# Shifting x by the mean of two feature tiles ahead of the block's product, and summing the block norm's squares on TensorE

## The reference

```python
def layer_norm(x, g, b):
    mu = jnp.mean(x, axis=-1, keepdims=True)
    var = jnp.mean(jnp.square(x - mu), axis=-1, keepdims=True)
    return (x - mu) * lax.rsqrt(var + LN_EPS) * g + b

def swiglu_ffn(x, w_gu, w_down):
    a, u = jnp.split(x @ w_gu, 2, axis=-1)
    return (jax.nn.silu(a) * u) @ w_down

for l in range(2):
    x = layer_norm(ALPHA * x + 0.5 * swiglu_ffn(x, ...), ln1_g[l], ln1_b[l])
    x = layer_norm(ALPHA * x + hybrid_mixer(x, ...), ln2_g[l], ln2_b[l])
    x = layer_norm(ALPHA * x + 0.5 * swiglu_ffn(x, ...), ln3_g[l], ln3_b[l])
```

```python
h = concatenate([meta, x])                      # 528 tokens
h = h + 0.5 * swiglu(rmsnorm(h, ffn1_norm), ...)
h = h + (differential attention | sparse attention over the 128 best keys) @ w_out
h = h + 0.5 * swiglu(rmsnorm(h, ffn2_norm), ...)
return h[:, 16:]
```

## Time and profile before

| | us |
|---|---|
| Median of three runs | 3179.1 |
| The profiled execution | 3178.52 |
| Its span, first to last instruction | 3177.1 |
| TensorE (PE) busy in it | 3067.3 |
| VectorE (DVE) busy | 1416.9 |
| ScalarE (ACT) busy | 1179.3 |
| GpSimd (POOL) busy | 372.4 |
| Mean granted clock of TensorE, as a share of full speed | 0.987 |

### The profile page before, as it was taken

How to read it: one execution, slowest core, us unless ns; L and a number is a source line. 1 busy time by engine, 2 the same in 40 slices (tenths; PEclk the granted TensorE clock), 3 DMA queues, 4 the chain that set the end, 5 groups by cost and what they waited for, 6 DMA issues and landing times.

```text
span 3177.1 us, 39372 instructions
## 1 busy us (share of the span) xinstructions
PE 3067.3 (97%) x16470; PEld 2564.3 (81%) x16470; DVE 1416.9 (45%) x2118; ACT 1179.3 (37%) x1914; POOL 372.4 (12%) x275
## 2 busy tenths in 40 slices
PE   9999999999999999999999999999999789799999
PEld 7888876888888888886788888899998657688888
DVE  3332455643335333375573333644323666554432
ACT  3322366433214222265552222522223456442321
POOL 0000133300001000033310001100014122110000
PEclk9999999999999999999999999999999899899999
DMA  4223221232232323331222233222233101122232
GB/s 157 93 92 92 97 87 54 67 107 93 91 97 78 107 93 89 97 108 54 67 81 99 93 91 95 69 91 91 84 93 108 34 27 41 34 87 93 98 88 80
DMA packets 76496, 269.62 MB, mean 85 GB/s; under 512 B 8720, under 2 KB 9008, under 8 KB 76064
## 3 DMA queue, kind: packets, MB, share of 16 engines
q1 hardware_dynamic: 74448, 260.08, 25.4%
q0 software_dynamic: 1872, 7.04, 0.7%
HBM read 264.97 MB, written 2.11 MB: 84 GB/s over the span
## 4 chain that ended last, share of the span: by engine, by line
PE 88%; DVE 6%; ACT 4%; issue 1%; DMA 0%; POOL 0%; SPq 0%; DVEq 0%; ACTq 0%
PE psum L339 25%; PE psum L342 24%; PE psum L345 24%; PE psum L400 3%; PE psum L412 2%; PE psum L362 1%; PE psum L358 1%; PE psum L360 1%; PE psum L636 1%; ACT w_hi L284 1%; DVE x_lo L703 1%; PE psum L2599 1%; DVE b_rank L2874 1%; ACT prob L1729 0%; DVE x L788 0%
## 5 line engine op out<-in xcount | busy, mean ns | idle before, releaser
L295 DVE TENSOR_TENSOR w_lo<-w_raw,w_hi 128x1024 fp32r<-128x1024 f32 (+1 forms) x442 | 551.5, 1250 | 1246.7 <-ACT w_hi L284 1246.6
L339 PE MATMUL psum<-x_hi,w_hi 128*128 128x512 f32 (+1 forms) x2792 | 967.9, 371 | 8.6 <-ACT neg_mean L2670 5.2
L342 PE MATMUL psum<-x_hi,w_lo 128*128 128x512 f32 (+1 forms) x2792 | 951.1, 365 | 0.0
L345 PE MATMUL psum<-x_lo,w_hi 128*128 128x512 f32 (+1 forms) x2792 | 946.3, 363 | 0.0
L284 ACT CAST w_hi<-w_raw 128x1024 fp32r<-128x1024 f32 (+1 forms) x490 | 504.0, 1029 | 1170.9 <-PE psum L345 1134.3
L339 PEld LDWEIGHTS psum<-x_hi,w_hi 128*128 128x128 f32 x2792 | 503.2, 190 | 114.2 <-issue 16.8
L342 PEld LDWEIGHTS psum<-x_hi,w_lo 128*128 128x128 f32 x2792 | 502.4, 190 | 87.7 <-issue 5.7
L345 PEld LDWEIGHTS psum<-x_lo,w_hi 128*128 128x128 f32 x2792 | 503.0, 190 | 84.4
L339 PE MATMUL psum<-h_hi_ffn,w_hi 128*128 128x512 f32 (+1 forms) x792 | 296.9, 375 | 0.0
L342 PE MATMUL psum<-h_hi_ffn,w_lo 128*128 128x512 f32 (+1 forms) x792 | 292.2, 369 | 0.0
L345 PE MATMUL psum<-h_lo_ffn,w_hi 128*128 128x512 f32 (+1 forms) x792 | 290.7, 367 | 0.0
(11 more groups left out here) (384 smaller groups left out, 3440.9 us busy)
## 6 DMA issues: line engine op xcount, KB each, us to landing
w_raw<-in_ffn_gu SPq DMA_DIRECT2D x176, 512.0 KB, 3.2
w_raw<-in_ffn_down SPq DMA_DIRECT2D x64, 512.0 KB, 3.5
w_raw<-in_w_in SPq DMA_DIRECT2D x44, 512.0 KB, 3.3
w_raw<-in_b_gate SPq DMA_DIRECT2D x44, 512.0 KB, 3.2
w_raw<-in_b_up SPq DMA_DIRECT2D x44, 512.0 KB, 3.3
w_raw<-in_b_down SPq DMA_DIRECT2D x32, 512.0 KB, 3.5
w_raw<-in_ffn_down SPq DMA_DIRECT2D x32, 384.0 KB, 3.1
w_raw<-in_b_in SPq DMA_DIRECT2D x24, 512.0 KB, 3.3
```

The costliest lines, as they stand in the source:

```text
L295: nc.vector.tensor_tensor(w_lo[s][:, 0:n], w_raw[r][:, 0:n], w_hi[s][:, 0:n].bitcast(F32), ALU.subtract).then_inc(*w_low_dve.inc(u))
L339: nc.tensor.matmul(out, w_h, hi[:, c], start=first and i == 0, stop=False)
L342: nc.tensor.matmul(out, w_l, hi[:, c], start=False, stop=False)
L345: done = nc.tensor.matmul(out, w_h, lo[:, c], start=False, stop=final and i == n - 1)
```

## The change

Four things, told by where they stand.

1. `FfnNorm` (four stages) and `MixerNorm` (two) take the early mean from x tiles 0 and 1 of the stage's input. GpSimd adds the two (one 512-wide add), TensorE multiplies the sum with the ones (one 512-wide float32 matmul) before up-piece 20, or at 18.6 in mixer_1's timetable; ScalarE negates and scales it; VectorE does `x = scale x - mean` on eight tiles as single instructions at every second step from s = 24 on, or from 19.2 to 21.3 in mixer_1. The additions of the product to x become plain ones. The shifts and the mean matmul of before go. In a feed-forward stage ScalarE now squares one tile per down tile, and GpSimd adds x tile and square in turn; the sum of x for tiles 0 to 6 comes whole from `z_sum`, where tile 6 had its own two 256-wide matmuls before.
2. At the end of mixer_1 two weight roundings on ScalarE stand one and two tiles earlier, and the sums of part 1 (`pe_sums(1)`) stand after the third instead of the second `x_hi`/`x_lo` step of the next stage.
3. `BlockNorm`: TensorE sums each squared tile as soon as it is there (16 float32 matmuls of 256 columns, accumulated), and the 14 GpSimd additions and the two 264-wide sums go. `x_hi` comes from the scaled x with a bias of its own (`shift2`), before x gets its bias. The mean is copied to SBUF and the centring reads it there. The meta tokens' part of the second norm (their `x_hi`, `x_lo`, squares, sum in eight 16-column matmuls, root) is done in the middle of ffn2_1.
4. The timetables of the mixers are written as starts and lags. In mixer_2 the sums come out in another order of rounding, by which some steps with the same number change places.

```diff
+    if leave.first_mean and i == 20:
+        leave.pe_first_mean()
...
+    if leave.before_block and s == 12:
+        leave.act_meta()
+    if leave.first_mean and s == 22:
+        leave.act_first_mean()
...
+    if leave.before_block and s == 15:
+        leave.dve_meta()
+    if leave.first_mean and 24 <= s < 24 + 2 * KT and s % 2 == 0:
+        leave.dve_shift((s - 24) // 2)
...
+            def pool_pair(self):
+                nc.gpsimd.tensor_tensor(neg_mean[:, TOK], x[:, 0, TOK], x[:, 1, TOK],
+                                        ALU.add).then_inc(*self.paired.inc(0))
+            def pe_mean(self, out):
+                pe.wait_ge(*self.paired.at(0))
+                nc.tensor.matmul(out, ones[:], neg_mean[:, TOK], start=True,
+                                 stop=True).then_inc(*self.mean_summed.inc(0))
+            def act_negate(self, product):
+                nc.scalar.mul(neg_mean[:, TOK], product,
+                              -self.scale / (2 * P)).then_inc(*self.negated.inc(0))
+            def dve_shift(self, m):
+                nc.vector.scalar_tensor_tensor(
+                    x[:, m, TOK], x[:, m, TOK], self.scale, neg_mean[:, TOK],
+                    ALU.mult, ALU.add).then_inc(*self.shifted.inc(m))
...
         class SecondNorm(LateRoot):
+            def pe_square(self, k, part):
+                if k == 0:
+                    pe.wait_ge(*self.first.mean_copied.at(part))
+                pe.wait_ge(*self.first.sq2.at((k, part)))
+                done = self.first.pe_sum(256, self.squares[k % 3], part, k == 0, k == KT - 1)
+                done.then_inc(*self.first.sq2_summed.inc((k, part)))
+            def pe_within(self, part, step):
+                k = step if step < 2 else step - 2
+                if part < 2 and step not in (2, 3):
+                    if k:
+                        self.pe_square(k - 1, part)
+                    elif part:
+                        self.pe_square(KT - 1, 0)
+                if (part, step) == (2, 0):
+                    self.pe_square(KT - 1, 1)
...
             def act_out(self, k, part):
                 act.wait_ge(*self.scaled.at((k, part)))
+                nc.scalar.activation(x_hi[:, k, c], x[:, k, c], ACT.Identity,
+                                     bias=shift2[:, k:k + 1], scale=gain(second.g, k))
                 nc.scalar.activation(x[:, k, c], x[:, k, c], ACT.Identity,
                                      bias=gain(self.b, k)).then_inc(*self.moved.inc((k, part)))
+                if k >= 3:
+                    act.wait_ge(*self.sq2_summed.at((k - 3, part)))
-                nc.scalar.mul(x_hi[:, k, full], x[:, k, full], gain(self.second.g, k))
-                if k >= 3:
-                    act.wait_ge(*self.total2.at((k - 2, part)))
...
         class MixerNorm
             def pe_within(self, part, k):
-                if (part, k) == (0, 1):
+                if (part, k) == (0, 2):
                     self.pe_sums(1)
             def end_dve(self):
-                for m in range(2):
-                    self.dve_shift(m)
                 for m in range(KT):
-                    if m + 2 < KT:
-                        self.dve_shift(m + 2)
+                    self.dve_second(m, 0)
                     if m == 1:
                         dve_split(self.u_second + OUT_PAIRS - 1)
-                    self.dve_second(m, 0)
...
         mixer_2
-                order += [(s, "b_score", i), ..., (s + 0.65, "b_turn", i), (s + 0.7, "b_inverse", i),
-                          (s + 0.75, "b_copy", i), (s + 0.95, "b_value", i), ...]
+ 'b': [('b_score', 0), ..., ('b_turn', 0.65), ('b_inverse', 0.7), ('b_copy', 0.75), ('b_value', 0.95), ...]
```

More of the change, by code:

```diff
@@ L1428, in timetable @@
[L1428 to L1441 removed]
+                    follow(ended(tile), "value", v)
@@ L2215, in timetable, with follow @@
                 order = []
+                def follow(at, what, item):
+                    order.extend((at + lag, step, item) for step, lag in LAGS_2[what])
                 for tile in range(IN_TILES_2):
```

429 lines of the change are left out of this document (220 added, 209 removed).

## The result

The changed kernel takes 3185.17 us in the median of 11 runs (3183.54 to 3188.99); the kernel before, on the same chip, 3179.1 (11 runs, 3172.67 to 3182.46). The ratio is 1.0020, with a 95% interval of 1.0011 to 1.0029: slower by 6 us, 3.5 to 9. I had forecast 3179 and no change. The measured time lies in the range of 3168 to 3188, but outside the forecast's own 3175 to 3184, and the change is not none.

The account below looks back on a forecast made before the run. TensorE was taken to bound the kernel. Terms 0 (feed-forward), +0.4 (seams), -0.6 (block norm), +1.6 (meta tokens) and -0.5 (mixer_2) gave +0.9 on 3178.52 us: 3179 us, no change, range 3168 to 3188, the forecast's own 3175 to 3184.

Parts of the forecast that it names:

- That TensorE bounds, and each part must be read where TensorE waits: Whole kernel: TensorE is busy 3067.3 of 3177.1 us, so an edit pays only where it waits or its work changes.
- Seams of mixer_1, +0.4: Two seams of mixer_1: the wait for L1252 stays, later part-1 sums add 0.2 us each; bounds -1.5 and +3.
- one rival only: Seams of mixer_1 do shorten: each gives back its 4.84 us wait and 1.0 us of clock, to 3168; chance 0.14.
- Meta tokens, +1.6: ffn2_1: eight matmuls of 16 columns that no pause of TensorE takes in cost 1.6 us.
- mixer_2, -0.5: mixer_2: seven neighbouring pairs change places on TensorE, -0.5 us in all; bounds -4 and +6.
- The block norm, -0.6: Block norm: 16 new sums lie mostly in TensorE's pauses and other steps come earlier, -0.6 us; bounds -2.3 and +6.
- the case that I had given 0.07: Block norm: filled pauses hold TensorE's full clock, -1.7 us more, to 3177.5; chance 0.07.
- the pace there is set by ScalarE and VectorE, one tile in 1.28 us: Block norm: a TensorE step with its sum takes 1.13 us at full clock, less than the 1.28 us pace.
- The prediction's own sign, a steady step over 1.3 us: Block norm: a steady step over 1.3 us was named as a sign that the forecast is wrong.
- The half microsecond that I took off: Block norm: `x_hi` before the bias has one ScalarE operation of 0.5 us less; TensorE enters L412 about 0.5 us sooner.
- The feed-forward stages, 0: Four feed-forward stages: TensorE's work is equal and single shifts find room on VectorE, 0 each; bounds together -1 and +3.
- The bound of 0.3%: Whole kernel: run to run, less than about 0.3%, 9.5 us, can't be told from no change; chance of within 0.73.

Follow-up runs that it names:

- the four kernels: One group: none of block norm with meta tokens, seam order, table 3180.1 us; seam order and table 3181.2; block norm and table 3182.6; block norm and seam order 3185.6.
- the ten with the long wait: Profiled executions of ten kernels, before and changed included, with the long wait at mixer_1's seam; granted clock behind it 0.56 in the changed kernel, 0.70 to 0.79 in nine others.

## Why the prediction was wrong

The forecast was no change, from terms of 0, +0.4, -0.6, +1.6 and -0.5. The steps that failed are three of them: the block norm, whose pace was read from the kernel before; the seams, where the later sums were taken as half covered; and the feed-forward stages, taken as equal work. The two others held.

- **That TensorE bounds, and each part must be read where TensorE waits:** right. The 6.9 us of its new busy time hold the meta matmuls (1.7), the sums, the slower reads and what the clock took and gave; its waits stayed the same in sum.
- **Seams of mixer_1, +0.4: the wait was right, its price was not.** That the wait hangs on the list behind the reciprocal is shown twice: 4.86 and 4.84 us of wait without the shifts, 2.33 with another order. (The count of that list left out the additions L1258 that stand behind each L1252; they don't change the argument.) The later sums, at 0.2 us a seam, were the wrong part: the times put 2.1 us (uncertainty 1.1) on the new order of both seams, and half covered was assumed without a row. The clock behind the wait was left out of the sum. I had it in one rival only, as 1.0 us to be won, from a window that ends at 630; from 627 to 634 it is (1 - 0.76) x 7 = 1.7. In the profiled pair, from the restart to 700 and 1700, the two seams cost 2.7 us together.
- **Meta tokens, +1.6:** right. In the view of TensorE after, 16 records for eight matmuls until the next product,

```profile
1739.31 1.85 PE L1231 MATMUL psum<-square,ones 128*128 128x16 f32 x16
1741.01 0.48 PE L392 MATMUL psum<-x_hi,w_hi 128*128 128x512 f32 x1
```

  1741.01 - 1739.31 = 1.70 us.
- **mixer_2, -0.5:** +5.2 on both sides of it, so 0.0 in that execution; the times of the four kernels give -1.0 (uncertainty 1.1), with which the term agrees.
- **The block norm, -0.6: this step failed.** The sums are mostly hidden, as I said. The clock stayed full: from 1985 to 2035 the granted clock was 0.93 in all six executions with the old block norm, 1.00 in six with the new one and 0.97 in the seventh, so the case that I had given 0.07 is the one that came. The rule of the Trainium skill that the prediction quotes ("TensorE: Matmul & The Clock Gate", Part 1) agrees with that. It should have been a gain. But "the pace there is set by ScalarE and VectorE, one tile in 1.28 us" was taken over for the changed kernel, in which ScalarE's instructions are other ones. The prediction's own sign, a steady step over 1.3 us, came: 1.34 to 1.41. 16 tiles at 0.1 to 0.15 us more are an estimate of 1.6 to 2.4 us; the stretch became 0.9 longer in each of the six traces with the new block norm and single sums, with the lower clock of before (worth up to 1.7 us in the second of its two stretches) no longer in it. The half microsecond that I took off because `x_hi` comes before the bias doesn't exist for `x_lo`, for which TensorE waits. By the times, this term and the meta tokens together were 3.5 us (uncertainty 1.1), where I had 1.0. TensorE's rows, from the last steps to the third piece:

```profile
2019.45 0.71 PE L453 MATMUL psum<-x_hi,w_hi 128*128 128x264 f32 x3
2021.01 0.63 PE L453 MATMUL psum<-x_lo,w_hi 128*128 128x264 f32 x3 [0.84 <-DVE x_lo L1286]
...
2024.71 0.71 PE L453 MATMUL psum<-x_hi,w_hi 128*128 128x264 f32 x3
2025.40 0.63 PE L453 MATMUL psum<-x_lo,w_hi 128*128 128x264 f32 x3
2025.86 0.59 PE L702 MATMUL psum<-square,ones 128*128 128x256 f32 x2
...
2027.51 2.31 PE L465 MATMUL psum<-x_hi,w_lo 128*128 128x264 f32 x16
...
2036.57 0.51 PE L392 MATMUL psum<-x_hi,w_hi 128*128 128x264 f32 x2 [0.68 <-DVE hid L619]
```

  L465 starts at 2027.51, less the 4.3 us by which the stage ended later 2023.2, where I had said half a microsecond before 2022.2.
- **The feed-forward stages, 0: this failed too, by two costs that the prediction didn't have.** "The work is equal" was right in instructions, and 1.7 us wrong in what they take, since a new tensor of 32 bytes moved `h_lo`. And the addition of x tiles 0 and 1 was looked at for its length only; it was never asked when it starts. It starts in the norm ahead of the stage, beside VectorE's longest list: 0.6 us after ffn2_0.
- **The sum.** Found by traces: 1.7 meta, 1.7 addresses, 0.6 addition, 0.9 block norm, 2.7 at the seams with what the lower clock took there, less 2.2 in the second mixer_1: 5.4 of the 5.6 us between the two profiled executions. The clock's share of the last two terms belongs to this pair of executions: among the ten with the long wait the changed kernel's had the least clock behind the first seam. That these shares cancel over many executions is not shown. The times, which don't depend on one execution, give 5.9 of 6.3 us with other weights: less for addresses and addition, more for block norm and meta tokens.
- **The bound of 0.3%** hid the rest. With 11 runs on either side the interval was 0.09% to each side, and a change of 0.2% was clear. The sum itself, +0.9, was small only because the terms that failed stood at 0, +0.4 and -0.6.

## What to carry to other kernels

When an engine waits at the end of another's list, count what stands in the list between the last pause and the release, and reorder that; taking work away ahead of the pause left the wait where it was (4.84 us), and the order behind it was worth about 7.6 us. When an instruction is moved or added, ask when its inputs are ready and not only whether it has time: an addition on an idle engine ran early, in the worst place. When it is moved ahead of another step, ask what still waits for both: `x_hi` came earlier, `x_lo` did not. And a pace read from the kernel before holds only while the instructions that set it stay as they are. Last, when several parts are undone in turn, undo them so that each is in half of the kernels: four kernels then weigh every part with all their runs.

## What was not expected of the hardware

- A float32r matmul of 512 columns stood 235 instead of 230 ns from its predecessor when its moving operand lay 32 bytes further on in SBUF, and 230 again at 256 bytes; others gained 1.1 ns by the same shift.
- One VectorE instruction with two SBUF inputs took 1.19 us and not 0.48 beside a GpSimd addition of 512 columns.
- A ScalarE pass of 256 columns with both scale and bias read from SBUF took 0.59 us where the one with a scale alone took 0.51.
- Behind the same pause of 4.8 us the granted clock of the next seven us was 0.56 in one profiled execution and 0.70 to 0.79 in nine others; the low stretch could begin before the pause ended. Behind a pause of 2.3 us it stayed full at five seams and fell at a sixth (0.58 from 1614 to 1618).
